# Second expert layer: fetched passes moved out of the gate stage, one gate part kept on chip, four value buffers

## What is computed

```python
def peer_ffn(h, w_query, sub_keys, u_tab, v_tab):
    q = (h @ w_query).reshape(B, L, PEER_HEADS, 2, PEER_QDIM // 2)
    s = jnp.einsum('blhtd,htnd->blhtn', q, sub_keys).astype(F32)
    ...
    idx = jnp.take_along_axis(cidx, pos, axis=-1)        # 8 heads x 16 of 16384 experts per token
    g = jax.nn.softmax(top, axis=-1).astype(h.dtype)
    ...
        act = jax.nn.gelu(jnp.einsum('td,tkd->tk', hx, u_tab[ix]))
        return jnp.einsum('tk,tkd->td', gx * act, v_tab[ix])
```

## Time and profile before

| | us |
|---|---|
| median of 3 runs (lowest, highest) | 2948.17 (2944.67, 2956.93) |
| the profiled execution's own time | 2943.05 |
| its span | 2941.2 |
| DVE busy | 2377.8 (81%) |
| PE busy | 2554.2 (87%) |
| ACT busy | 1197.0 (41%) |
| POOL busy | 644.6 (22%) |
| SP's queue of loads, share of the 16 DMA engines | 46.9% |
| POOL's queue of fetched rows | 18.5% |

### The profile page before, as it was taken

One profiled execution on the slowest core, in us unless ns is written; L12 is line 12 of the kernel. 1 busy time (PEld: TensorE's weight loads), 2 busy tenths in 40 slices (PEclk: granted clock), 3 DMA queues, 4 the chain that ended last, 5 costly groups with the idle time before them and its releaser, 6 DMA issues. The chain is left out here.

```text
span 2941.2 us, 44148 instructions
## 1 busy us (share of the span) xinstructions
PE 2554.2 (87%) x16181; PEld 2260.1 (77%) x16181; DVE 2377.8 (81%) x4626; ACT 1197.0 (41%) x1806; POOL 644.6 (22%) x486
## 2 busy tenths in 40 slices
...
DVE  7877679977999999999962655589968788888877
...
PEclk9987899999999999999988998898989999999988
DMA  5720333579998989989941313244889999999985
GB/s 216 276 70 26 144 128 121 190 277 321 305 314 298 314 308 308 313 293 293 304 148 66 114 57 130 86 138 164 317 327 351 336 352 354 355 340 345 333 309 192
DMA packets 333353, 708.38 MB, mean 241 GB/s; under 512 B 172848, under 2 KB 175696, under 8 KB 326368
## 3 DMA queue, kind: packets, MB, share of 16 engines
q1 hardware_dynamic: 272896, 466.60, 46.9%
q0 software_dynamic: 55360, 201.38, 18.5%
...
## 5 line engine op out<-in xcount | busy, mean ns | idle before, releaser
L1996 PE MATMUL pe_s<-hl_hi,pq_uh 128*128 128x320 f32 (+2 forms) x2304 | 718.2, 312 | 48.9 <-DVE pq_ul L163 25.1
L1997 PE MATMUL pe_s<-hl_lo,pq_uh 128*128 128x320 f32 (+2 forms) x2304 | 706.9, 307 | 0.0
L1998 PE MATMUL pe_s<-hl_hi,pq_ul 128*128 128x320 f32 (+2 forms) x2304 | 705.3, 306 | 0.0
L2079 PE MATMUL peer_acc<-val_vh,val_w 128*128 128x512 f32 x2048 | 613.8, 403 | 85.6 <-DVE val_w L163 85.3
L2079 PEld LDWEIGHTS peer_acc<-val_vh,val_w 128*128 128x128 f32 x2048 | 386.2, 193 | 181.2 <-DVE val_vl L163 103.3
L1996 PEld LDWEIGHTS pe_s<-hl_hi,pq_uh 128*128 128x128 f32 x2304 | 450.8, 196 | 72.0 <-issue 38.4
L1997 PEld LDWEIGHTS pe_s<-hl_lo,pq_uh 128*128 128x128 f32 x2304 | 451.0, 196 | 8.5
L1998 PEld LDWEIGHTS pe_s<-hl_hi,pq_ul 128*128 128x128 f32 x2304 | 450.2, 195 | 0.0
L2253 POOL DMA_INDIRECT pe_frow<-in_peer_rows,pe_fidx x192 | 234.1, 1219 | 876.1 <-DVE pe_frow L2413 813.3
L2253 POOL DMA_INDIRECT pe_frow<-in_peer_v,pe_fidx x192 | 286.0, 1489 | 496.8 <-DVE pe_fh L2429 232.5
L2197 ACT ACTIVATE val_vh<-val_vr 128x1024 fp32r<-128x1024 f32 x256 | 270.6, 1057 | 259.3 <-DMA val_vr<-in_peer_v 229.0
...
## 6 DMA issues: line engine op xcount, KB each, us to landing
pq_ur<-in_peer_u SPq DMA_DIRECT2D x256, 512.0 KB, 4.5
val_vr<-in_peer_v SPq DMA_DIRECT2D x256, 512.0 KB, 5.7
...
val_mrow<-in_ada_rows SPq DMA_DIRECT2D x56, 512.0 KB, 7.4
val_gr<-gates SPq DMA_DIRECT2D x128, 160.0 KB, 5.8
pq_ur<-in_w_query SPq DMA_DIRECT2D x32, 512.0 KB, 3.5
s_wv<-val_out SPq DMA_DIRECT2D x32, 512.0 KB, 7.9
val_gr<-gates SPq DMA_DIRECT2D x128, 128.0 KB, 7.1
```

The lines of the kernel that those rows point to most:

```text
L1996: pe.matmul(o, r32(uh[:, b, k]), r32(hi[:, k, a:T]), start=k == 0, stop=False)
L1997: pe.matmul(o, r32(uh[:, b, k]), r32(lo[:, k, a:T]), start=False, stop=False)
L1998: mm = pe.matmul(o, r32(ul[:, b, k]), r32(hi[:, k, a:T]), start=False, stop=k == KC - 1)
L2079: mm = pe.matmul(acc[:, 2 * t + c, :], r32(lhs[:, b, w]), r32(rhs[:, b, c * 512:(c + 1) * 512]), start=False, stop=False, skip_group_check ...
```

## The change

Layer 0's plan is the old one, but for the order of SP's loads in a slot. In layer 1 (`held` = 1, `each` = 4, `values` = 4, `early` = 0):

- no fetched pass in the gate stage; all 256 are spread over the 128 slots, two in each;
- the last of the four gate parts is kept in its half of `gate_stg` and not stored; `apply` becomes two multiplications, 192 tokens with loaded gates and 64 with kept ones;
- the other three parts are loaded for four slots at a time (128 x 3 x 1024 bytes, 384 KB);
- four value buffers for two, the two new ones where the one-hot tiles were; values 2 and 3 are loaded ahead of `x`;
- in each slot SP issues the values ahead of the table (in both layers).

```diff
-PLANS = Plan(64, [3] * 12 + [2] * 2, 0), Plan(128, [2] * 16, 32)
+PLANS = Plan(64, [3] * 12 + [2] * 2, 0, 1, 2, 0), Plan(128, [2] * 16, 1, 4, 4, 0)
...
+        self.held, self.each, self.values = held, each, values
+        self.stored = self.parts - held
+        self.odd_stored = (self.parts + 1) // 2 - held
...
+        spare_vr = x.sb("more_vr", [P, VALUES - 2, D]) if VALUES > 2 else None
...
+            def gate(m):
+                src = gates_dram[0:plan.stored, :, m * EACH:(m + 1) * EACH, :]
+                sp.dma_start(gr[:, m % 2], src.rearrange("h p a c -> p h (a c)")).then_inc(gload[m % 2], 16)
...
                 if n == RING:
-                    sp.wait_ge(gst1, 16 * ((PARTS + 1) // 2))
+                    sp.wait_ge(gst1, 16 * plan.odd_stored)
+                    if plan.held:
+                        sp.wait_ge(gst2, 16 * (PIECES - 1) * plan.odd_stored)
...
             sp.wait_ge(gated, CHUNKS)
+            for n in range(2, VALUES):
+                value(n)
             sp.dma_start(cx.x[:], d["x_kept"]).then_inc(xback, 16)
 
             def slot(z):
                 b = z.n % 2
+                if z.has(VALUES):
+                    sp.wait_ge(vlow, z.n + 3)
+                    value(z.n + VALUES)
                 if z.has(RING + 2):
                     sp.wait_ge(ulow2, z.n + (RING - LOW + 1))
                     table(z.n + (RING + 2), b)
                 if z.has(2):
-                    sp.wait_ge(vlow, z.n + 3)
-                    value(z.n + 2, b)
-                    sp.wait_ge(applied, z.n + 1)
-                    if z.n + 2 >= SOON:
-                        sp.wait_ge(gst2, 16 * ((PIECES - 1) * ((PARTS + 1) // 2 - 1) + 2))
-                    gate(z.n + 2, b)
+                    if (z.n + 1) % EACH == 0 and z.n + 1 + EACH < NB:
+                        sp.wait_ge(applied, z.n + 1)
...
+                        gate((z.n + 1) // EACH + 1)
...
-                if c >= full:
+                if full <= c < plan.stored * (full + 1) + full:
                     store_piece(c, (c - full) // (full + 1), (c - full) % (full + 1))
...
-            act.wait_ge(evacd, CHUNKS)
-            store_rest(PARTS - 1, SOON, SOON + REST)
+            if not plan.held:
+                act.wait_ge(evacd, CHUNKS)
+                store_rest(PARTS - 1, SOON, SOON + REST)
...
             def apply(z, ahead):
-                v.tensor_tensor(a, a, gr[:, b].rearrange("p h c -> p (h c)"), ALU.mult).then_inc(applied, 1)
+                a = A[:, z.place(ahead), 0:held].rearrange("p (h c) -> p h c", c=HALF)
+                ins = v.tensor_tensor(a, a, gr[:, m % 2, :, at:at + HALF], ALU.mult)
+                if plan.held:
+                    a = A[:, z.place(ahead), held:TOKENS]
+                    ins = v.tensor_tensor(a, a, stg[:, 1, n], ALU.mult)
+                ins.then_inc(applied, 1)
```

48 lines of the change are left out of this document (26 added, 22 removed).

## The result

The changed kernel takes **2853.32 us** (median of 4 runs, 2847.38 to 2855.33) where the kernel before takes 2948.35 (2944.67 to 2956.93). The ratio is 0.967, 95% interval 0.9644 to 0.9696: faster, by 95 us. The prediction was 2894 us with a range from 2868 to 2930. The direction was right, the size was not: the gain is nearly twice the forecast, and outside the range.

A forecast was written before the change was run, and what follows sets the result against it. The prediction took DVE to bound layer 1's gate stage and DMA its value-stage slots with a table. Its terms, -33 - 10 + 0 - 7 + 1 = -49 us from 2943, gave 2894 us, range 2868 to 2930.

The forecast's parts named there:

- What bounds the kernel now: Opening step: DVE bounds layer 1's gate stage, and DMA sets the value stage's slots with a table, 6.04 us each.
- C: Value-stage slots with a table: DMA time changes by +0.02 us a slot, so 0 us; bounds -6 and +24.
- rival 1: The queues gain more: share reaches 0.985, both transition stalls go, -69 us in all, 2874 us; chance 0.17.
- rival 4: Value stage: tables land late behind values and gates, slots of 7.14 us, +48 us in all, 2991 us; chance 0.04.
- A: Layer 1's gate stage: 32 passes leave it, -33 us; bounds -36.6 and -16.
- Rival 3: Gate stage goes over to PE at a partly lower clock, saving 16 us instead of 33, 2911 us; chance 0.10.
- B: Transition: the last gate part isn't stored, -10 us; bounds 0 and -17.1.
- D: Slots without a table: DMA share rises to 0.97, 4.64 us a slot, -7 us; bounds +1 and -12.
- E: End of the value stage: the last two slots end with four passes for three, +1 us.
- Rival 2: Value stage: bytes bind, not pieces, at 347 and 330 GB/s; slots grow, -6 us in all, 2937 us; chance 0.08.
- The one test that I named for the value stage: Wrong if the value stage, first `apply` to last pass, is more than 20 us longer than its 738 us.

The follow-up runs named there:

- d_first: The kernel before with only the order of SP's loads in a slot changed, to gates, values, table: 2889.29 us, ratio 0.9829.
- d_first_early0: d_first with the 32 early passes also taken out of layer 1's gate stage: 2866.36 us, ratio 0.9737.
- u_pieces: The change with each gate load for four slots issued as four loads of 256-byte pieces at the same time: 2852.88 us.
- u_gatefirst: The change with gates loaded slot by slot in 256-byte pieces, issued ahead of values and table: 2845.37 us, ratio 0.9669.
- u_early32: The change with its 32 early passes put back into the gate stage: 2871.25 us, ratio 0.9746.
- x_first16: u_gatefirst with 16 passes put back into the gate stage, one a step, taken from the slots without a table: 2839.76 us, ratio 0.9653.
- r_change: The change itself, repeated on the same chip as r_first16: 2852.93 us.
- r_first16: x_first16 repeated, on the same chip as r_change: 2843.65 us.

## Why the prediction was wrong

**"What bounds the kernel now" is where it failed.** "The waits name the queue [...] So a slot of 483/80 = 6.04 us is set by DMA". The waits name loads. I read them with the share of 0.97 as a full queue, and didn't look at when the loads were asked for. The slot was set by one loop: a gate buffer free at 2296.47, its load issued at 2301.24 behind SP's wait for the table, landed at 2311.54, where the stall of the earlier trace rows ends; in the mean of 66 slots 12.1 us from an `apply` to the next in its buffer, for two slots. That the share was high did not mean that nothing more could pass: d_first moved 374 GB/s at a share of 1.01, d_first_early0 398 at 1.04.

**C, forecast 0, measured -32.6 us.** The sum of prices (5.86 and 5.88 us of DMA a slot) was a sum of records' times, and no floor: the changed kernel's records add up to a share of 1.01, and its slot is bound by PE at 5.63 us. DVE's 5.35 us was foreseen right (measured 5.36). Of the -0.32 us for the new gate load, 0.15 were for fewer bytes (0.62 to 0.47) and 0.17 for larger pieces (0.47 to 0.30). As records' times these were sized right: 48 ns for a piece of 1 KB and 18 for one of 256 bytes, 0.29 us a slot in the change and 0.43 in u_pieces. As time of the slot u_pieces has the pieces at nothing. Even the bound was wrong: a share of 0.98, or 0.985 in rival 1, gave -6, since I held the share for the only thing that could rise. The rule of the Trainium skill that stood beside it ("DMA: Bandwidth & Descriptors", "Why small descriptors are slow") would have made the value stage some 16 us longer than my sum has it, and it came out shorter than the sum. Whether the rule holds on the DMA engines no run here decides: u_pieces shows nothing of the pieces in the time (2852.88 for 2853.32), since PE covers it.

In rival 4 I worked out just this kind of loop for the tables (landing, ACT, DVE, over two buffers: 4.0 us a slot, hidden). The same two-slot sum for the gates, with their issue times from SP's timeline, gives 5.9 us, and would have shown that the kernel's bound was a loop with over 3.5 us of queueing in it (3.55 from 2302.99 to 2306.54), which the change takes off the path by asking for gates four slots at a time. With PE's 459.89 busy us in 80 slots, 5.75, as what is late next, C would have been some -23 us.

**A, forecast -33, measured -34.7.** Right: steps of 5.96 us, DVE busy for 94.59 of 96 us. Rival 3 fell: the granted clock rose from 0.90 to 0.97, with PE busy for 81.55 of 96 us where it had been for 96.06 of 133.

**B, forecast -10, measured -15.7.** Right in kind, near its bound of -17.1: the 4.19 MB are gone, and of the two stalls only parts are left. Between d_first_early0 (71.8) and u_gatefirst (61.0) the kept part, with the value buffers, is worth 10.8 us, the -10 of the forecast; d_first shows another 4.5 that go by the order alone (73.1 for 77.6).

**D, forecast -7, measured -11.6**, within its bounds of +1 and -12, at the far end. The sum came near for reasons that I didn't have. With 1.75 passes a slot, as before, the order alone takes these slots from 4.90 to 4.53 us (d_first) and the change's buffers and kept part to 4.19 (u_early32); the quarter pass more brings them back to 4.60, that is 16 us in 39 slots. 39 x 0.25 x 1.2 = 11.7 of them are DVE's own work, and the rest is a longer wait for fetched rows (9.0 us in the change, 2.4 in u_early32). The share did rise, to 0.96, but it wasn't what the slot went by: the waits for gates, 32 us in these 39 slots before, are gone in the change.

**E, forecast +1, measured +4.8.** The passes behind the last `apply` take 6.85 us for 5.5. Most of the other 3.4 us are in the final norm, where DVE waits longer for a square root by ACT (9.91 us for 7.01); I did not find out why.

**The rivals.** Rival 1 (2874) was the nearest, and its reason, queues that run further ahead, was half of the truth: they did run ahead, but what they had been held back by was SP's list and not their share. Rival 2, a ceiling of bytes at 347 GB/s, is refuted by 392 to 398 GB/s held over some 450 us. The Trainium skill's figure of about 358 GB/s for a core ("DMA: Bandwidth & Descriptors", "Bandwidth") is passed as well; its other figure, about 425 for a core alone ("HBM Reference", "Specifications (TRN2)"), is not. Rival 4 did not come: in 80 slots ACT waits 7.2 us in all for `pq_ur`, and DVE 6.8 for `pq_uh`. The one test that I named for the value stage looked only for a loss (20 us longer than 738); from the 9th to the 128th `apply` it came out 44 us shorter, and only the slot that I had named, 6.0 to 6.1 us for 5.63 measured, shows the error.

**What the parts are worth**, along one chain of ratios, each in parts of 2948 us: the order of the loads 50 us (d_first, 0.9829), no passes in the gate stage 27 (d_first_early0, 0.9737), the kept part with four value buffers 20 (u_gatefirst, 0.9669), 16 of the passes back in the gate stage 5 (x_first16, 0.9653). The change reaches the first by another way, four slots to a load. The intervals are up to 0.3% wide on each side, so a step under some 8 us isn't told apart from nothing. That holds for the last one, which rests on the stretches alone; r_change and r_first16 tell x_first16 from the change, and not from u_gatefirst. That gates first and slot by slot (2845) beat the change (2853) was not tried on one chip, and 6 us of it lie ahead of the gate stage. Two value buffers with the kept part and the gates first were not tried at all. Both stay open.
